# Seven block products in place of eight on every second weight slab of the shared values

## The reference, cut to what matters

```python
x = _layernorm(DEEPNORM_ALPHA * x + y, ln_g[layer], ln_b[layer])
if layer == N_A - 1:
    k_sh = (x @ w_k_shared).reshape(B, T, 2 * DIFF_HEADS, DIFF_HEAD_DIM).transpose(0, 2, 1, 3)
    v_sh = (x @ w_v_shared).reshape(B, T, DIFF_HEADS, 2 * DIFF_HEAD_DIM).transpose(0, 2, 1, 3)
```

## Time and profile before

| what | value |
|---|---|
| timed runs, median (lowest to highest) | 2400.02 us (2399.64 to 2400.69) |
| span of the profiled execution, first to last instruction | 2399.3 us |
| median of the timed runs less that span | 0.7 us |
| PE busy | 2361.7 us, 98% of the span |
| DVE busy | 1534.4 us, 64% |
| ACT busy | 1209.0 us, 50% |
| POOL busy | 17.1 us, 1% |
| share of the `vs` stage (727.3 to 816.8 us) | 89.5 us, 3.7% |

### The profile page before, as it was taken

The page is one execution under the profiler, slowest core; times in us unless marked ns, Lnnn a source line. Parts: engine busy times, 40 slices in busy tenths (PEclk is TensorE's granted clock), DMA queues, the critical chain, the costliest instruction groups (busy, mean ns, idle before and its releaser), DMA issues.

```text
span 2399.3 us, 49369 instructions
## 1 busy us (share of the span) xinstructions
PE 2361.7 (98%) x20503; PEld 2229.2 (93%) x20503; DVE 1534.4 (64%) x1893; ACT 1209.0 (50%) x1590; POOL 17.1 (1%) x36
## 2 busy tenths in 40 slices
PE   9999999989999999999999999999999999999998
PEld 9999799879998899999999999999999888999886
DVE  8588588566774455657799875656745444555445
ACT  5586563354464466755644346465544333444343
POOL 0000000000000000000000000000000000000000
PEclk9999999999999999999999999999999999999999
DMA  9355566325556644564566565655666666666664
GB/s 285 116 184 175 178 191 187 99 74 179 180 169 187 189 151 158 180 201 141 158 193 179 165 184 167 185 179 150 199 199 173 191 190 186 185 184 183 193 186 148
DMA packets 216554, 419.90 MB, mean 175 GB/s; under 512 B 17056, under 2 KB 19440, under 8 KB 215648
## 3 DMA queue, kind: packets, MB, share of 16 engines
q1 hardware_dynamic: 207520, 397.98, 54.5%
q0 software_dynamic: 2560, 10.59, 1.4%
q10 hardware_dynamic: 6288, 8.61, 1.3%
HBM read 410.84 MB, written 6.29 MB: 174 GB/s over the span
## 4 chain that ended last, share of the span: by engine, by line
PE 92%; DVE 5%; ACT 2%; issue 1%; DMA 0%; DVEq 0%; ACTq 0%
PE ps L504 28%; PE ps L505 28%; PE ps L506 28%; DVE wlo L369 1%; PE ps L724 1%; ACT whi L365 1%; PE ps L652 1%; PE ps L638 1%; PE ps L732 0%; PE ps L988 0%; DVE regions L1978 0%; PE ps L869 0%; DVE act_lo L2292 0%; PE ps L749 0%; PE ps L1003 0%
## 5 line engine op out<-in xcount | busy, mean ns | idle before, releaser
L369 DVE TENSOR_TENSOR wlo<-wraw,whi 128x1024 fp32r<-128x1024 f32 x752 | 916.4, 1223 | 786.9 <-ACT whi L365 785.6
L365 ACT ACTIVATE whi<-wraw 128x1024 fp32r<-128x1024 f32 x752 | 793.4, 1058 | 1040.3 <-PE ps L506 1021.7
L504 PE MATMUL ps<-act_hi,whi 128*128 128x256 f32 (+2 forms) x4480 | 1274.8, 285 | 10.5 <-DVE act_lo L2292 7.4
L505 PE MATMUL ps<-act_lo,whi 128*128 128x256 f32 (+2 forms) x4480 | 1261.2, 282 | 0.0
L506 PE MATMUL ps<-act_hi,wlo 128*128 128x256 f32 (+2 forms) x4480 | 1259.8, 281 | 0.0
L504 PEld LDWEIGHTS ps<-act_hi,whi 128*128 128x128 f32 x4480 | 842.7, 188 | 17.9 <-issue 12.6
L505 PEld LDWEIGHTS ps<-act_lo,whi 128*128 128x128 f32 x4480 | 845.4, 189 | 1.1
L506 PEld LDWEIGHTS ps<-act_hi,wlo 128*128 128x128 f32 x4480 | 843.0, 188 | 0.0
L505 PE MATMUL ps<-wlo,regions_r 128*128 128x512 f32 x512 | 202.2, 395 | 0.0
L504 PE MATMUL ps<-whi,regions_r 128*128 128x512 f32 x512 | 202.2, 395 | 0.0
L506 PE MATMUL ps<-whi,regions_r 128*128 128x512 f32 x512 | 202.2, 395 | 0.0
(11 more groups left out here) (369 smaller groups left out, 1477.6 us busy)
## 6 DMA issues: line engine op xcount, KB each, us to landing
wraw<-in_a_w_in SPq DMA_DIRECT2D x128, 512.0 KB, 3.8
wraw<-in_w_up SPq DMA_DIRECT2D x128, 512.0 KB, 3.8
wraw<-in_w_down SPq DMA_DIRECT2D x128, 512.0 KB, 3.7
wraw<-in_w_in SPq DMA_DIRECT2D x112, 512.0 KB, 3.8
wraw<-in_b_w_qg SPq DMA_DIRECT2D x64, 512.0 KB, 4.0
wraw<-in_a_w_out SPq DMA_DIRECT2D x32, 512.0 KB, 4.1
wraw<-in_w_k_shared SPq DMA_DIRECT2D x32, 512.0 KB, 3.8
wraw<-in_w_v_shared SPq DMA_DIRECT2D x32, 512.0 KB, 4.2
```

The costliest lines, as they stand in the source:

```text
L365: nc.scalar.activation(whi[:, q % RING], wraw[:, q % RING], ACT.Copy).then_inc(hi_ready, 1)
L369: nc.vector.tensor_tensor(wlo[:, q % RING], wraw[:, q % RING], whi[:, q % RING].bitcast(F32), ALU.subtract).then_inc(lo_ready, 1)
L504: mm(o, hi_s, hi_m, start=first, stop=False, skip_group_check=True)
L505: mm(o, hi_s, lo_m, start=False, stop=False, skip_group_check=True)
```

## The change

In the four groups of `vs`, the odd slabs (1, 3, 5, 7) are multiplied in another way. Such a slab is the product of a 2 x 2 block matrix of activations (two token blocks of 128 by two row blocks of 128) with a 2 x 2 block matrix of weights (two row blocks by two column halves of 256). Before, this took eight block products, done as 12 matmuls of 512 columns. Now it takes Strassen's seven products (in the variant with shared sums), each three matmuls of 256 columns: 21 matmuls of 256 columns. Even slabs stay as they were.

- For each odd slab GpSimd makes four sums and differences of the weight's quarters in three instructions (`weight_sums`: 512, 256 and 256 numbers on each partition, each waiting for the one before). ACT then rounds three raw quarters (768 numbers) and, when the sums are there, the four sums (1024); DVE makes the two low parts (768 and 1024).
- The four sums of the activations' blocks are made once, on DVE during the last groups of `ks` (`token_sums`, four instructions of 512 numbers), and split on ACT (two of 1024) and DVE (two of 1024).
- A group now fills four PSUM banks: two with what goes straight into the result, two with four side terms. After a group ACT copies the side banks out (`side_banks`, 1024 numbers, in the place of the copy to `vS`), GpSimd adds them up (`product_sums`: 256, 256 and 512 numbers), and DVE adds the result to the two direct banks and writes `vS` (`joined`, 1024 numbers, after the split of slab 6 of the next group). TensorE waits for `joined` of the group two before.
- In GpSimd's list the `product_sums` of a group stand behind the `weight_sums` of slab 3 of the next group and ahead of those of slab 5.
- The loop of two passes becomes four groups written out.
- To stay within the number of semaphores, several signals of other stages are merged into common ones with counts (`lam_ready` and `lam_done` into `lam_dve`, and so on); what waits for what there stays the same. `acc_act` loses the four counts of `vs`.

The core of the diff:

```diff
         def split_hi(act, G, q):
+            if in_vs(G, q):
+                return split_hi_sums(act, G, q)
...
+        def split_hi_sums(act, G, q):
+            act.wait_ge(raw_loaded[q % RING], 16 * (2 * G + 1 + q // RING))
+            act.wait_ge(slab_used, SLABS * G + q - RING + 1)
+            nc.scalar.activation(quarters(whi[:, q % RING])[:, 0:3], quarters(wraw[:, q % RING])[:, 0:3], ACT.Copy).then_inc(hi_ready, 1)
+            act.wait_ge(S["t_ready"], odd_slab(G, q) + 1)
+            nc.scalar.activation(thi[q // 2 % 2], tf[q // 2 % 2], ACT.Copy).then_inc(S["thi_ready"], 1)
+
+        def weight_sums(eng, G, q):
+            raw, i, n = quarters(wraw[:, q % RING]), q // 2 % 2, odd_slab(G, q)
+            eng.wait_ge(raw_loaded[q % RING], 16 * (2 * G + 1 + q // RING))
+            eng.wait_ge(slab_used, SLABS * G + q - RING + 1)
+            nc.gpsimd.tensor_tensor(tf[i][:, 0:2], raw[:, 1:3], raw[:, 3:4].broadcast_to([P, 2, T]), ALU.subtract).then_inc(S["t_part"], 1)
+            eng.wait_ge(S["t_part"], 2 * n + 1)
+            nc.gpsimd.tensor_tensor(tf[i][:, 2], raw[:, 1], tf[i][:, 1], ALU.add).then_inc(S["t_part"], 1)
+            eng.wait_ge(S["t_part"], 2 * n + 2)
+            nc.gpsimd.tensor_tensor(tf[i][:, 3], raw[:, 0], tf[i][:, 2], ALU.subtract).then_inc(S["t_ready"], 1)
+
+        def split_lo_sums(dve, G, q):
+            raw, i, n = quarters(wraw[:, q % RING]), q // 2 % 2, odd_slab(G, q)
+            dve.wait_ge(hi_ready, SLABS * G + q + 1)
+            nc.vector.tensor_tensor(quarters(wlo[:, q % RING])[:, 0:3], raw[:, 0:3], quarters(whi[:, q % RING])[:, 0:3].bitcast(F32), ALU.subtract)
+            dve.wait_ge(S["thi_ready"], n + 1)
+            nc.vector.tensor_tensor(tlo[i], tf[i], thi[i].bitcast(F32), ALU.subtract).then_inc(lo_ready, 1)
+
+        def product_sums(eng, n):
+            z = side_terms[n % 2]
+            eng.wait_ge(S["z_ready"], n + 1)
+            nc.gpsimd.tensor_tensor(z[:, 1], z[:, 0], z[:, 4], ALU.add).then_inc(S["z_part"], 1)
+            eng.wait_ge(S["z_part"], 2 * n + 1)
+            nc.gpsimd.tensor_tensor(z[:, 2], z[:, 1], z[:, 2], ALU.add).then_inc(S["z_part"], 1)
+            eng.wait_ge(S["z_part"], 2 * n + 2)
+            nc.gpsimd.tensor_tensor(z[:, 1:4:2], z[:, 1:3], z[:, 6:7].broadcast_to([P, 2, T]), ALU.subtract).then_inc(S["z_summed"], 1)
...
+            for n in range(4):
+                for q in (1, 3, 5, 7):
+                    weight_sums(pool, G0["vs"] + n, q)
+                    if n and q == 3:
+                        product_sums(pool, n - 1)
+            product_sums(pool, 3)
...
-            with pe.Fori(0, 2) as i:
-                for s in range(2):
-                    pe.wait_ge(acc_act, 2 * i + (ACC_ACT["vs"] + s - 1))
-                    wm_group(2 * i + (G0["vs"] + s), [bank(2 * s), bank(2 * s + 1)], ahi, alo)
+            def seven(G, q, b0):
...
+                three(half(2, 0), *x_of(2 * q + 1, 0), *w_of(2), first=opens, last=last)
+                three(half(0, 0), *x_of(2 * q, 0), *w_of(0), first=False, last=last)
+                three(half(0, 1), *s_of(3), *w_of(1), first=False, last=last)
+                three(half(1, 0), *x_of(2 * q, 1), *t_of(3), first=False, last=last)
+                three(half(3, 0), *s_of(2), *t_of(0), first=opens, last=last)
+                three(half(2, 1), *s_of(1), *t_of(2), first=False, last=last)
+                three(half(3, 1), *s_of(0), *t_of(1), first=False, last=last, sig=slab_used)
+
+            for n in range(4):
+                if n < 2:
+                    pe.wait_ge(acc_act, ACC_ACT["ks"] + 3 + n)
+                else:
+                    pe.wait_ge(S["vs_done"], n - 1)
+                G, b0 = G0["vs"] + n, 4 * (n % 2)
+                for q in range(SLABS):
+                    pe.wait_ge(lo_ready, SLABS * G + q + 1)
+                    if q % 2:
+                        if n == 0 and q == 1:
+                            pe.wait_ge(S["sums_made"], 3)
+                        seven(G, q, b0)
+                        continue
...
             for s in range(8):
                 pe.wait_ge(acc_act, ACC_ACT["q"] + s - 1)
+                if s < 2:
+                    pe.wait_ge(S["vs_done"], 3 + s)
...
-            evac_stage("vs", 4, lambda s: st.do(a(vS[:, :, s * GW:(s + 1) * GW], two(s), ACT.Copy), sig["acc_act"]))
+            def side_banks(n):
+                if n >= 2:
+                    act.wait_ge(S["vs_done"], n - 1)
+                b2 = 4 * (n % 2) + 2
+                st.do(a(side_terms[n % 2].rearrange("p (h b x) t -> p b h x t", h=2, b=2)[:, :, :, 0, :],
+                        ps[:, b2:b2 + 2, :].rearrange("p b (h t) -> p b h t", h=2), ACT.Copy), sig["z_ready"])
+            evac_stage("vs", 4, side_banks)
...
+            def joined(n):
+                dve.wait_ge(S["z_summed"], n + 1)
+                b0 = 4 * (n % 2)
+                st.do(tt(vS[:, :, n * GW:(n + 1) * GW], side_terms[n % 2][:, 0:4].rearrange("p (b h) t -> p b (h t)", b=2), ps[:, b0:b0 + 2, :],
+                         ALU.add), sig["vs_done"])
+            for n in range(4):
+                group_slabs(dve, split_lo, G0["vs"] + n, (lambda u, n=n: joined(n - 1) if u == 2 else None) if n else None)
```

More of the change, by code:

```diff
@@ L165, in program @@
             xh_ready n_hi q4_ready th_ready acc_act
[L166 to L170, removed]
+            acc_dve extra_loaded meta_loaded grp_loaded lam_dve lam_exp sc_mm
+            sc_read sc_ready e_ready at_ready att_mm attT_ready o_mm ostd_ready on_ready ot_mm ot_ready in_ready
+            in_hi ssq ssum sstd meta_act meta_mm meta_dve cv_a pool_d pool_mm
+            pool_y conv_c cs_mm xc_ready sqc_ready cv_mm conv_act cn_ready conv_y f_sq f_hi
+            f_ready out_cols ysq
+            sums_made sums_hi t_part t_ready thi_ready z_ready z_part z_summed vs_done""".split()
         S = {n: sem(n) for n in names}
@@ L327, in program @@
         metaU = R[:, 1, C:C + KT * META].rearrange("p (k t) -> p k t", k=KT)
+        blocks4 = lambda t_: t_.rearrange("p (s n) -> p s n", s=4)
+        SEVEN = 7 * T
+        tf = [blocks4(R[:, 0, 1024 * i:1024 * (i + 1)]) for i in range(2)]
+        tlo = [blocks4(RR[:, 0, 1024 * i:1024 * (i + 1)]) for i in range(2)]
+        thi = [blocks4(RR[:, 0, 2048 + 1024 * i:3072 + 1024 * i]) for i in range(2)]
+        by_pair = lambda t_: t_.rearrange("p (c s t) -> p c s t", c=4, s=4)
+        sums, sums_lo, sums_hi = by_pair(R[:, 3, 0:2048]), by_pair(RR[:, 3, 0:2048]), by_pair(RR[:, 3, 2048:4096])
+        side_terms = [R[:, 6, 2048 * i:2048 * i + 2048].rearrange("p (s t) -> p s t", t=T) for i in range(2)]
+        quarters = lambda t_: t_.rearrange("p a n -> p (a n)").rearrange("p (s n) -> p s n", s=4)
+        odd_slab = lambda G, q: 4 * (G - G0["vs"]) + q // 2
+        in_vs = lambda G, q: isinstance(G, int) and G0["vs"] <= G < G0["vs"] + 4 and q % 2 == 1
         sa, sgb, mT = four_k(0), four_k(1), four_k(2)
@@ new lines, in _ @@
+            for n in range(4):
[11 more added lines that the diff above has]
+                        continue
+                    for kk in range(2):
+                        for tb in range(2):
+                            k = 2 * q + kk
+                            three(bank(b0 + tb), block(ahi[:, k, :], tb), block(alo[:, k, :], tb), whi[:, q % RING, kk], wlo[:, q % RING, kk],
+                                  first=q == 0 and kk == 0, last=False, sig=slab_used if kk == 1 and tb == 1 else None)
@@ L1529, in ln0_act @@
                     ln0_chunk((t - 11) // 2)
+                if t in (25, 26):
+                    c2 = slice(2 * t - 50, 2 * t - 48)
+                    act.wait_ge(S["sums_made"], 1)
+                    st.do(a(sums_hi[:, c2], sums[:, c2], ACT.Copy), sig["sums_hi"])
                 if t in (14, 23):
@@ L2371, in ln0_dve, with token_sums @@
                               sig["ks_fixed"] if e and k else None)
-            slabs = lambda name, n: [group_slabs(dve, split_lo, G0[name] + s) for s in range(n)]
+            def token_sums(t):
+                x_ = H.rearrange("p (c k) t -> p c k t", k=4)
+                a11, a12, a21, a22 = x_[:, :, 3, 0:P], x_[:, :, 2, 0:P], x_[:, :, 3, P:T], x_[:, :, 2, P:T]
+                s1, s2, s3, s4 = (sums[:, :, j, :] for j in range(4))
+                if t == 22:
+                    st.do(tt(s1, a21, a22, ALU.add))
+                    st.do(tt(s3, a11, a21, ALU.subtract))
+                if t == 23:
+                    st.prev(2)
+                    st.do(tt(s2, s1, a11, ALU.subtract))
+                if t == 24:
+                    st.prev()
+                    st.do(tt(s4, a12, s2, ALU.subtract), sig["sums_made"])
+                if t in (27, 28):
+                    c2 = slice(2 * t - 54, 2 * t - 52)
+                    dve.wait_ge(S["sums_hi"], t - 26)
+                    st.do(tt(sums_lo[:, c2], sums[:, c2], sums_hi[:, c2].bitcast(F32), ALU.subtract), sig["sums_made"])
             for s in range(4):
```

(8 more changed lines are left out.)

75 lines of the change are left out of this document (44 added, 31 removed).

## The result

Four executions of the changed kernel lie between 2412.23 and 2415.68 us, median 2414.18; the kernel before, run beside it, has a median of 2400.36. The ratio is 1.0057 [1.0043, 1.0071]: 13.8 us slower, where 2395.1 was forecast. The time lies inside the stated range (2394.6 to 2421), and in the 2409 to 2427 us of the first rival, GpSimd and VectorE keeping each other out.

A forecast was written before the change was run, and what follows sets the result against it. TensorE was taken to bound the kernel: the 2399.3 us span less 4.9 for shorter matmuls gives 2394.4, plus 0.7 by which timed runs exceed the span, 2395.1 us, all else hidden. The stated range was 2394.6 to 2421.

The forecast's parts named there:

- the first rival: GpSimd and VectorE instructions reading SBUF in `vs` can't run at once, so their times add: 2409 to 2427 us, chance 0.40.
- What bounds the kernel: TensorE, busy 2361.7 of 2399.3 us; `vs` is bound by matmuls, with operands ready 5.81 us early.
- the gain of 4.93 us: In `vs`, 21 matmuls of 256 columns save 0.308 us per odd slab, over 4 groups x 4 odd slabs.
- the work added on DVE, ACT, in `ks` and in the waits of PE is hidden: DVE 14.8 and ACT 13.0 us fit a group of 21.2; activation sums in `ks` and PE's new waits cost nothing.
- the formula 3p + 4.6 against 13.2 us: After each of three group hand-overs, time until slab 5 is ready against when PE wants it; p may be 2.86.
- At p = 2.2 all is hidden: With a GpSimd set of 2.2 us, PE waits nowhere in `vs`, neither at ordinary odd slabs nor at hand-overs.
- p: Time of one GpSimd set of three dependent instructions over 1024 numbers; taken as 2.2 us, ends 1.3 and 3.1.
- the hidden case: GpSimd's sums in `vs` cost PE nothing: 2395.1 us, own range 2394.6 to 2397.2, chance 0.42.
- two marks: Exclusion signs: DVE's splits exceed 1.22 us or POOL's equal-size instructions differ; PE waits at odd slabs all along `vs`.
- the third case: GpSimd slow by itself, p 3.1 to 3.9: PE idle only at slab 5 of groups 1 to 3; 2397 to 2404, chance 0.14.
- the 5.4 us that the prediction allowed at an ordinary odd slab: The longest a GpSimd set may take at an ordinary odd slab, with PE back after 7.93 us.
- Loads: Hidden: A buffer's next load in `vs` lands 8.8 us after PE's end, before PE frees the buffer at 10.6.

The follow-up runs named there:

- the first experiment: Changed kernel with GpSimd's six sum instructions replaced by memsets of the same outputs, sums left out: 2395.62 us, ratio 0.9981 to the kernel before.
- the second experiment: Changed kernel with GpSimd's sums replaced by memsets as long as a set of sums takes by itself: 2397.46 us, ratio 0.9987 to the kernel before.
- the third experiment: Changed kernel with DVE's low parts in `vs` made as raw times a constant, one operand read: 2400.78 us, ratio 1.0002 to the kernel before.
- the fourth experiment: Changed kernel with GpSimd's product sums placed behind the weight sums of slab 5 instead of slab 3: 2411.25 us, ratio 1.0055 to the kernel before.

## Why the prediction was wrong

*Right.* What bounds the kernel, the gain of 4.93 us, and that the work added on DVE, ACT, in `ks` and in the waits of PE is hidden: the first experiment shows them together. The place where PE would feel a slow GpSimd, slab 5 behind each of three hand-overs, and the formula 3p + 4.6 against 13.2 us: with the measured lengths it gives 4.1, 3.6 and 3.9 us late, and 4.2, 3.6 and 4.2 were measured. That the time lies inside the stated range is no merit of the forecast: the range was stretched to reach a rival, and the forecast's own, 2394.6 to 2397.2, was missed by 17 us.

*The step that failed* is "At p = 2.2 all is hidden", and the term in it is p. It had one number for GpSimd's set, the same whether DVE works or not.
- By itself a set takes 2.89 us, near the upper end of 1.3 to 3.1 and just above the 2.86 allowed. The estimate from the Trainium skill (GPSIMD Engine Reference, section 3.1), 2.7, was nearer than the 2.2 chosen between the rows. This error alone is worth the 1 to 2 us of the second experiment.
- Beside DVE a set takes 4.6 to 5.1 us, above the upper end: up to three waits for DVE, of 0.8, 1.0 and 0.7 us in the set at 751.87. That is the other 17 to 18 us, clock included. The rows of the memset could not show it, as the prediction said; choosing the hidden case over the rival, 0.42 to 0.40, was choosing by rows that did not bear on the question.

*The rival that came true* is mutual exclusion, in its strict form. The Trainium skill (SBUF — State Buffer, "Who interferes with whom") had stated it for a VectorE instruction with two SBUF inputs and a GpSimd one that reads SBUF: the later one is blocked until the first is done, and a GpSimd instruction that only writes is free. The rows agree with both clauses, to 0.03 us and at DVE's unchanged 1.22. The rival's price, splits and sets added up, is 13.6 + 5 x 2.9 = 28.1 against 21.2, 6.9 us a group or 28 over the stage; 19.1 came. Groups 1 to 3 last 27.4, 26.5 and 27.6 us, near that sum. Group 0, in whose time GpSimd does four sets (25.2 by the same sum), lasts 22.2; why it stays 3 us below is not worked out. Of its two marks one held (DVE's splits stretch), the other only in part: PE was to wait all along the stage, and it waited mainly at the hand-overs, the mark of the third case, GpSimd slow by itself. Both marks are one chain: the turns lengthen p, and the place with the least room shows it first. No set is longer than the 5.4 us that the prediction allowed at an ordinary odd slab; the 2.86 of the hand-overs were exceeded.

*Not foreseen:* 4.6 of the 19.1 us are not waits, but slab 5 at a lower clock behind them. And "Loads: Hidden" holds only up to p = 4.0: with p = 5 the prediction's own sum is 5 + 2.4 + 4.2 = 11.6 us against the 10.6 at which PE frees the buffer. So it came: the three sets that began 0.9 to 1.1 us late behind a load are those of the slabs for which PE had its three short waits.

## What to carry to other kernels

Before work is moved to GpSimd because it is idle, look at what VectorE does in the same microseconds: where both read SBUF operands in the forms measured here, add their times instead of laying them side by side, and add them at the place with the least room. If VectorE has the room itself, it did here in 1.6 us what took GpSimd 2.89 alone and 4.6 to 5.1 in turns. When both lengths of a pair seem to stretch by half, compare single starts and ends before speaking of a shared rate.

## What the runs showed of the hardware

- DVE and GpSimd take turns by whole instructions. The one behind waits until the other's is over, and then needs its own length less 0.13 us (104 of 107 lengths in the changed kernel's stage, 105 of 108 in the third experiment; the others are `joined`). This holds for DVE's `tensor_tensor` with both operands in SBUF and for its one-operand multiply by a constant (1024 fp32 in 0.69 us), not for a GpSimd memset (DVE's split 1.22 us beside memsets of 0.96), and not for DVE with an operand in PSUM (1.21 us beside GpSimd). Why the one-operand multiply takes turns, no run here shows.
- GpSimd adds 512 and 512 fp32 numbers in 1.29 us and 256 and 256 in 0.72, with 0.08 us from one to a waiting next one.
- After TensorE had waited for slab 5 of group 1 (4.1 us idle), its granted clock in the next 3.87 us was 0.63: matmuls of 256 columns followed each other every 0.21 us at first, the lower level of 1.2 GHz, and every 0.12 from 771.9 us on. The three waits of 3.6 to 4.2 us cost another 1.4 to 1.6 us each in this way. Behind the 2.8 us waits of the fourth experiment the clock was 0.60 to 0.72, behind the 1.7 us wait of the third 1.00.

```profile
769.58 0.41 PE L570 MATMUL ps<-whi,act_lo 128*128 128x256 f32 x1
769.79 0.41 PE L568 MATMUL ps<-whi,act_hi 128*128 128x256 f32 x1
...
772.13 0.28 PE L568 MATMUL ps<-regions_r 128*128 128x256 f32 x1
772.25 0.28 PE L569 MATMUL ps<-regions_r 128*128 128x256 f32 x1
```
